# Interleaving the operation streams of attention and of the recurrent and SSD groups, with separate PSUM banks, in a two-layer hybrid decoder

## Chip, cores and metric

One Trainium2 chip, all 8 NeuronCores, each working on two of the 16 sequences with no communication. The metric is the device time of the slowest core in microseconds; less is better.

## The reference

The model has two layers over x of shape (16, 4096, 1024), float32. Each layer mixes tokens and then channels.

```python
proj = h @ w_in[l]          # 1024 -> 4368 columns, split among three head groups
# A recurrent group: GeLU gate * RG-LRU(causal width-4 conv), 512 channels:
#   a = exp(-8 r softplus(-lam)); u = sqrt(1 - a^2) * (i * x);  h_t = a_t h_(t-1) + u_t
# B Mamba-2 SSD group: conv + SiLU, 16 heads of 64, state 128, chunks of 128:
y_diag = einsum('bgcls,bcsghp->bclghp', cb[:, :, None] * decay, x)
states = einsum('bclgn,bclghp->bcghpn', bc, x * decay_states[..., None])
y_off = einsum('bclgn,bcghpn->bclghp', cc, prev) * out_decay[..., None]
#   then + D x, * SiLU(z), RMSNorm by group, 1024 channels
# C attention: window 128, 8 query and 2 key/value heads of 64, one sink per head:
p = exp(logits - m); probs = p / (sum(p) + exp(sink - m)); out = probs @ vv
# the three outputs (2048 columns) go through w_out, then
h = layer_norm(alpha * h + mix)
# PEER: top-16 of 128^2 experts for each of 8 heads, gated GELU neurons
h = layer_norm(alpha * h + peer(h))
```

## The kernel before

Every operation is recorded in one program-wide list by `Prog.op`, with the names of what it reads and writes. From these names come the waits: an operation waits on the semaphore of the engine that made what it reads, and of the last readers of what it overwrites. PSUM is also tracked by bank: `bank_of` maps names to banks, a reader waits for the bank's last matmul, and a matmul waits for all readers of its bank since then. `emit` gives each engine its operations in the order in which they were recorded, so each of the five queues (PE, DVE, ACT, POOL, SP) runs in program order.

After an initial normalization and a conversion of the expert tables, each layer has a mixer phase (`mixer_phase`, L319) and a PEER phase (`peer_phase`, L593), with a barrier between them. The change lies in the mixer phase alone. It goes over 2 sequences of 32 chunks of 128 tokens, that is 64 chunks for each layer, and each chunk does these steps, in this order on every engine:

1. The chunk of h is loaded (L415), cast (L416), transposed on PE (L418) and copied (L419). The load overwrites the single buffer `h`, which L587 of the chunk before reads, and its SP queue stands behind the store L590.
2. Projections (L425 to L446), their copies, SiLU of z (L449, L450), softplus for dt (L452 to L455).
3. Attention, L457 to L483: for each of 8 heads two logit matmuls (L461, L462) into bank 5 or 6, mask (L464, DVE), maximum (L465), scaling and negation (L466, L467), a memset of the sum (L468), Exp with accumulated sum (L469, ACT), Exp of the sink (L470, ACT), sum and reciprocal (L471, L472), two transposes into bank 7 (L474), their copy (L475, ACT), two matmuls with v into bank 4 (L478, L479), and the scaled copy (L480, DVE). Most small buffers (`lm`, `pb`, `pTt`, columns of `sm`) are single. Then four transposes (L482) and a copy into ymT (L483).
4. Causal convolution (L487 to L491): 64 DVE operations on 16 blocks of 128 channels.
5. RG-LRU (L493 to L520), four blocks one after the other: cast (L495), gate matmuls (L498) into bank 5 or 6, Tanh (L499, L500), a DVE chain (L501 to L508), Ln and Exp (L509, L510), scan (L513), the gate's GeLU with POOL (L515 to L517) and Tanh (L518), and the product (L519, L520). ACT loads a function table where Ln and Tanh follow each other.
6. SiLU of the 12 SSD blocks (L523 on ACT, L524 on DVE, one buffer `th`), transposes (L526, L529) into bank 7, and small steps (L531 to L542).
7. SSD for each of two groups (L543 to L578): decay matrix through fp32 matmuls (L548) into banks 2 and 3, mask (L551, POOL), Exp (L552), product (L554), matmuls (L557) into bank 0 or 1, L560 into bank 4 or 6, L553 and L562 into bank 5, state update, gating, RMSNorm. Then transposes L580 and copy L581.
8. Output projection (L585) into banks 0 and 1, residual (L587), LayerNorm (`ln_rows`, L257), store (L590).

Of the kernel before, what the change touches and what calls it, by code (L numbers as in the profile page):

```python
# [22 lines left out]
class Prog:  # L23
# [161 lines left out]
def bc(ap, shape):  # L185
    return ap.to_broadcast(list(shape))
# [132 lines left out]
def mixer_phase(nc, P, es_outer, E, l):  # L319
    op = P.op  # L320
    g = E
    NSEQ, S, NCH = g["NSEQ"], g["S"], g["NCH"]
    PB, PT = g["PB"], g["PT"]
    ident, iof, triu, ones, smask, amask, AMK = g["ident"], g["iof"], g["triu"], g["ones"], g["smask"], g["amask"], g["AMK"]
    hs0, hs1 = g["hs0"], g["hs1"]
    lnst, ln_rows, epsb = g["lnst"], g["ln_rows"], g["epsb"]
    with contextlib.ExitStack() as st:
# [4 lines left out]
        Wg = sb("Wg", [128, 4, 2, 128], BF16)  # L332
# [3 lines left out]
        rgc = sb("rgc", [128, 4, 4])  # L336
# [65 lines left out]
        PTv = PT[:].rearrange("p (k e) -> p k e", k=8)  # L402

        for sq in range(NSEQ):
# [6 lines left out]
            for c in range(NCH):  # L411
# [44 lines left out]

                for hd in range(8):  # L457
# [28 lines left out]

                for b in range(16):  # L487
                    eng = "dve"
                    op(eng, lambda e, b=b: e.tensor_scalar(out=xc[:, b, :], in0=X[:, b, 0:128], scalar1=cw[:, b, 0:1], scalar2=cw[:, b, 4:5], op0=ALU.mult, op1=ALU.add), reads=["X", "Xh0", "cw"], writes=[("xc", b), "wgs"])
                    for k in range(1, 4):  # L490
                        op(eng, lambda e, b=b, k=k: e.scalar_tensor_tensor(out=xc[:, b, :], in0=X[:, b, k:k + 128], scalar=cw[:, b, k:k + 1], in1=xc[:, b, :], op0=ALU.mult, op1=ALU.add), reads=["X", "Xh0", "cw", ("xc", b)], writes=[("xc", b)])  # L491

                for b in range(4):  # L493
                    A, B_, C_, D_, E_, F_, G_, H_ = [t1[i] for i in range(8)]
                    op("act", lambda e, b=b: e.copy(out=xcb[:], in_=xc[:, b, :]), reads=[("xc", b)], writes=["xcb"])  # L495
                    bk = 5 + b % 2
                    for gi in range(2):
                        op("pe", lambda e, b=b, gi=gi, bk=bk: e.matmul(PB[bk][:, gi * 128:(gi + 1) * 128], lhsT=Wg[:, b, gi, :], rhs=xcb[:], start=True, stop=True), reads=["Wg", "xcb"], writes=[("lg", bk, gi)])  # L498
                    op("act", lambda e, b=b, bk=bk: e.activation(out=A[:], in_=PB[bk][:, 0:128], func=AF.Tanh, bias=rgc[:, b, 0:1], scale=0.5), reads=[("lg", bk, 0), "rgc"], writes=["tA", ("seg", 0), ("seg", 1)])  # L499
                    op("act", lambda e, b=b, bk=bk: e.activation(out=B_[:], in_=PB[bk][:, 128:256], func=AF.Tanh, bias=rgc[:, b, 1:2], scale=0.5), reads=[("lg", bk, 1), "rgc"], writes=["tB", ("seg", 0), ("seg", 1)])  # L500
# [42 lines left out]
                for g_ in range(2):  # L543
# [9 lines left out]
                    op("pe", lambda e, g_=g_: e.matmul(PB[5][:, 0:128], lhsT=xsb[:, 8 + g_, :], rhs=xsb[:, 10 + g_, :], start=True, stop=True), reads=[("xsb", 8 + g_), ("xsb", 10 + g_)], writes=["pb5", ("lg", 5, 0)])  # L553
                    op("dve", lambda e: e.tensor_tensor(out=MT[:], in0=seg[:], in1=bc(PB[5][:, 0:128].unsqueeze(1), [128, 8, 128]), op=ALU.mult), reads=[("seg", 0), ("seg", 1), "pb5"], writes=["MT"])  # L554
# [353 lines left out]
```

How the kernel before makes its waits and increments, by code:

```python
            def run(engname, eng):  # L134
                waited = {}
                for o in ops:
                    if o["eng"] != engname:
                        continue
                    need = {}
                    for d in o["deps"]:
                        s, v = semval(ops[d])
                        key = id(s)
                        if need.get(key, (None, 0))[1] < v:
                            need[key] = (s, v)
                    for key, (s, v) in need.items():
                        if waited.get(key, 0) >= v:
                            continue
                        waited[key] = v
                        eng.wait_ge(s, v)
                    ins = o["fn"](eng)
                    if o["dma"] is not None:
                        lst = ins if isinstance(ins, (list, tuple)) else [ins]
                        assert len(lst) == o["ndma"], (len(lst), o["ndma"])
                        s, _ = semval(o)
                        for x in lst:
                            x.then_inc(s, 16)
                    elif o["sig"]:
                        s, _ = semval(o)
                        ins.then_inc(s, 1)
                if engname == "sp":
                    for n, s in dsem.items():
                        eng.wait_ge(s, self.dma_cum[n])
```

## Time and profile before

| | |
|---|---|
| median of 3 runs | 64667.56 us (64598.34 to 64866.73) |
| profiled execution, its own time | 64709.24 us |
| its span, slowest core (core 1) | 64707.7 us |
| spans of all cores | 64189.3 to 64707.7 us |
| busy PE / DVE / ACT / POOL, core 1 | 27332.0 / 28776.0 / 21378.7 / 10896.5 us (42% / 44% / 33% / 17%) |

The span is the time from the first to the last instruction of the core. A busy share is an average over phases that have different limits, so it is read by stretch. The granted clock is the share of TensorE's full clock of 2.4 GHz that was granted; 0.50 is the lower level of 1.2 GHz.

### The profile page before, as it was taken

The page shows a single profiled execution, that of the slowest core. Times are in us where ns is not written, and L with a number is a line of the kernel's source. Part 1 is how long each engine was busy: PE and PEld are TensorE (multiplying, and loading weights), DVE is VectorE, ACT ScalarE, POOL GpSimd, SP SyncE. Part 2 cuts the span into 40 slices and gives each one's busy share as a digit, 9 for nine tenths or more (in the row PEclk, how much of TensorE's full clock was granted, in tenths as well). Part 3 has the DMA queues.
Part 4 walks back from the last instruction along what each step waited for, and adds up shares of the span by engine and source line. Part 5 has one row for each costly group of instructions (what it writes and reads, how often), then busy time and mean ns, then how long its engine had stood idle before and what let it go on. Part 6 is the DMA issues. An engine that isn't in the chain of part 4 may idle for free.

```text
span 64707.7 us, 666132 instructions; the slowest of 8 cores (64189.3 to 64707.7 us)
## 1 busy us (share of the span) xinstructions
PE 27332.0 (42%) x192896; PEld 17066.1 (26%) x192896; DVE 28776.0 (44%) x65858; ACT 21378.7 (33%) x30175; POOL 10896.5 (17%) x12169
## 2 busy tenths in 40 slices
PE   0122222222456565555562222222245555565556
PEld 0011111111233333333331111111123333333333
DVE  1033333433555555555543433333455555555554
ACT  0122222222344444444432222222234444444444
POOL 2111111111121222222221111111112221222222
PEclk9955555555676777777775555555567777777778
DMA  3500000000233333333340000000023333333334
GB/s 130 179 5 6 6 6 6 5 6 6 88 129 129 129 131 131 131 130 132 131 149 15 5 6 6 6 6 6 5 71 130 131 132 130 131 131 131 131 134 152
DMA packets 2497687, 5211.34 MB, mean 81 GB/s; under 512 B 155808, under 2 KB 155808, under 8 KB 2490016
## 3 DMA queue, kind: packets, MB, share of 16 engines
q1 hardware_dynamic: 2494112, 5168.71, 23.6%
q8 instruction: 1629, 26.69, 0.2%
q14 instruction: 1946, 15.94, 0.1%
HBM read 4866.33 MB, written 301.99 MB: 80 GB/s over the span
## 4 chain that ended last, share of the span: by engine, by line
PE 28%; DVE 28%; ACT 18%; issue 11%; DMA 9%; POOL 4%; DVEq 1%; SPq 1%; ACTq 0%; POOLq 0%
PE pb L821 8%; ACT WT_p L782 8%; PE pb L831 7%; DMA Ug_p<-UTs 5%; DVE xc L491 3%; PE pb L425 3%; PE pb L585 2%; DMA ust<-peer_u 2%; PE pb L548 1%; PE pb L675 1%; DVE seg L505 1%; DVEq L149 1%; ACT ge_p L822 1%; ACT L509 1%; ACT L518 1%
## 5 line engine op out<-in xcount | busy, mean ns | idle before, releaser
L821 PE MATMUL pb<-h1T_p,Ug_p 128*128 128x256 bf16 x65536 | 9784.6, 318 | 8077.9 <-ACT ge_p L822 5328.6
L823 POOL TENSOR_TENSOR gW_p<-ge_p,WT_p 128x256 bf16<-128x256 bf16 x8192 | 6310.7, 777 | 26455.2 <-ACT ge_p L822 19428.0
L821 PEld LDWEIGHTS pb<-h1T_p,Ug_p 128*128 128x128 bf16 x65536 | 7139.9, 112 | 10467.3 <-issue 8751.7
L831 PE MATMUL pb<-Vg_p,gW_p 128*128 128x512 bf16 x32768 | 8657.7, 425 | 4.4 <-DMA Vg_p<-VBs 4.2
L822 ACT ACTIVATE ge_p<-pb 128x256 bf16<-128x256 f32 x8192 | 3341.5, 421 | 8694.4 <-PE pb L821 7202.8
L782 ACT CAST WT_p<-pt 128x512 bf16<-128x512 f32 x2048 | 5000.2, 2441 | 1567.7 <-PE pb L780 1508.8
L768 DVE TENSOR_TENSOR ohA_p<-iocb,selT_p 128x1024 bf16<-128x1024 bf16 x2048 | 2626.3, 1282 | 5981.3 <-PE pb L780 3181.7
L782 ACT CAST WT_p<-pb 128x512 bf16<-128x512 f32 x2048 | 4988.3, 2436 | 241.7 <-PE pb L831 3.4
L770 DVE TENSOR_TENSOR ohB_p<-iocb,selT_p 128x2048 bf16<-128x2048 bf16 x2048 | 4876.3, 2381 | 0.0
L831 PEld LDWEIGHTS pb<-Vg_p,gW_p 128*128 128x128 bf16 x32768 | 3462.1, 107 | 4335.2 <-issue 2627.7
L498 PE MATMUL pb<-xcb,Wg 128*128 128x128 bf16 x1024 | 190.5, 289 | 6615.7 <-ACT xcb L495 6615.7
L769 DVE TENSOR_TENSOR ohA_p<-ohA_p,selT_p 128x1024 bf16<-128x1024 bf16 x2048 | 2758.1, 1347 | 219.7 <-DVE ohA_p L768 8.3
L841 DVE SCALAR_TENSOR_TENSOR sc_p<-hq_p,pb 128x512 f32<-128x512 f32 x256 | 176.1, 688 | 5796.0 <-PE pb L831 4912.8
L515 POOL TENSOR_TENSOR seg<-gate 128x128 f32<-128x128 f32 x512 | 203.9, 398 | 14675.5 <-DVE ymT L520 12874.1
L491 DVE SCALAR_TENSOR_TENSOR xc<-X,cw,xc 128x128 f32<-128x128 f32 x6144 | 2158.4, 351 | 659.2 <-DVE xc L491 14.2
L693 DVE MAX8 V_p<-sc_p 128x8 f32<-128x128 f32 x2048 | 567.4, 277 | 3107.1 <-ACT sc_p L685 3105.7
L498 PEld LDWEIGHTS pb<-xcb,Wg 128*128 128x128 bf16 x1024 | 69.8, 104 | 6736.5 <-issue 6736.5
L548 PE MATMUL pb<-daU,ones 128*128 128x512 f32 x1024 | 941.1, 1074 | 2012.6 <-DVE daU L546 2012.6
L474 PE MATMUL pt<-ident,pb 128*128 128x128 bf16 x2048 | 379.9, 288 | 3337.5 <-ACT pb L469 3337.5
L425 PE MATMUL pb<-hT,Wi 128*128 128x128 bf16 x25600 | 1720.4, 238 | 121.9 <-DVE hT L419 121.9
L425 PEld LDWEIGHTS pb<-hT,Wi 128*128 128x128 bf16 x25600 | 1701.7, 108 | 152.3 <-issue 152.3
L780 PE MATMUL pt<-ohA_p,ohB_p 128*128 128x64 bf16 x16384 | 974.5, 210 | 1145.1 <-DVE ohB_p L770 1101.4
(244 smaller groups left out, 42165.5 us busy)
## 6 DMA issues: line engine op xcount, KB each, us to landing
Ug_p<-UTs SPq DMA_DIRECT2D x2048, 1024.0 KB, 8.2
Vg_p<-VBs SPq DMA_DIRECT2D x2048, 1024.0 KB, 5.5
ust<-peer_u SPq DMA_DIRECT2D x256, 512.0 KB, 4.0
vst<-peer_v SPq DMA_DIRECT2D x256, 512.0 KB, 4.8
hq_p<-hs SPq DMA_DIRECT2D x256, 512.0 KB, 6.2
UTs<-utb SPq DMA_DIRECT2D x256, 256.0 KB, 2.1
VBs<-vbf SPq DMA_DIRECT2D x256, 256.0 KB, 2.6
h<-hs SPq DMA_DIRECT2D x128, 512.0 KB, 3.8
```

The source lines that it names most:

```text
L425: op("pe", lambda e, b=b, c0=c0, kc=kc: e.matmul(PB[bank][:, b * 128:(b + 1) * 128], lhsT=Wi[:, kc, c0:c0 + 128], rhs=hT[:, kc, :], start= ...
L491: op(eng, lambda e, b=b, k=k: e.scalar_tensor_tensor(out=xc[:, b, :], in0=X[:, b, k:k + 128], scalar=cw[:, b, k:k + 1], in1=xc[:, b, :], o ...
L548: op("pe", lambda e, j=j: e.matmul(PB[2 + j][:, :], lhsT=ones[:], rhs=daU[:, 4 * j:4 * j + 4, :].rearrange("p a b -> p (a b)"), start=True ...
L585: op("pe", lambda e, hf=hf, kc=kc: e.matmul(PB[hf][:, :], lhsT=ymT[:, kc, :], rhs=Wo[:, kc, 512 * hf:512 * (hf + 1)], start=(kc == 0), sto ...
L768: op("dve", lambda e: e.tensor_tensor(out=ohA[o_][:], in0=ioh, in1=bc(selT[sl][:, 0, toks].unsqueeze(2), [128, 16, 64]), op=ALU.is_equal), ...
L769: op("dve", lambda e: e.tensor_tensor(out=ohA[o_][:], in0=ohA[o_][:], in1=bc(selT[sl][:, 2, toks].unsqueeze(2), [128, 16, 64]), op=ALU.mul ...
L770: op("dve", lambda e: e.tensor_tensor(out=ohB[o_][:], in0=iob, in1=bc(selT[sl][:, 1, toks].unsqueeze(2), [128, 16, 128]), op=ALU.is_equal) ...
L782: op("act", lambda e, tk0=tk0, dst_ps=dst_ps: e.copy(out=WT[:, i0c, tk0:tk0 + 8].rearrange("p i t -> p t i"), in_=dst_ps[:, :].rearrange(" ...
L821: op("pe", lambda e, gl=gl, kc=kc, ab=ab: e.matmul(PB[ab][:, 0:TT], lhsT=Ug[gs_][:, gl, kc, :], rhs=h1T[sl][:, kc, :], start=(kc == 0), st ...
L822: op("act", lambda e, ab=ab: e.activation(out=ge[ab][:], in_=PB[ab][:, 0:TT], func=AF.Gelu), reads=[("pp", ab)], writes=[f"ge{ab}"])
L823: op("pool", lambda e, ab=ab, gl=gl, eb=eb: e.tensor_tensor(out=gW[gs_][:, gl, :], in0=ge[ab][:], in1=WT[:, eb, :], op=ALU.mult), reads=[f ...
L831: op("pe", lambda e, gl=gl, sub=sub, hf=hf, bk=bk: e.matmul(PB[bk][:, :], lhsT=gW[gs_][:, gl, sub * 128:(sub + 1) * 128], rhs=Vg[gs_][:, g ...
```

## The change

Three things are done.

`Prog` gets a recording mode: while `chain` is a list, `op` only appends its arguments to it. `merge(a, b)` then records two such lists into the program, taking from the one that is behind in proportion of its length; the order inside each list stays. The dependencies are worked out at this point, in the merged order.

In `mixer_phase`, steps 3 (attention, with L482 and L483) go into `_chA`, and steps 4 to 7 (convolution to L581) into `_chB`; after L581 the two are merged. Steps 1, 2 and 8 stay outside.

The PSUM banks of `_chB` change. Gate matmuls L498: bank 5 or 6 to bank 0. Transposes L526, L529 and L580: bank 7 to bank 1, through a bf16 view `PT1`. L531 and L532: bank 6 to 3. L553: bank 5 to 0. L557: bank `g_` to 1 for both groups. L560: bank 4 or 6 to 2. L562: bank 5 to 3. L548 keeps banks 2 and 3, and attention its banks 4 to 7. The instructions that read these banks are changed alike, and so are the names by which waits are found. No operation is added or taken away.

```diff
+    chain = None
+
+    def merge(self, a, b):
+        na, nb = len(a), len(b)
+        ia = ib = 0
+        while ia < na or ib < nb:
+            if ib >= nb or (ia < na and ia * nb <= ib * na):
+                self.op(*a[ia]); ia += 1
+            else:
+                self.op(*b[ib]); ib += 1
+
     def op(self, eng, fn, reads=(), writes=(), dma=None, ndma=1):
+        if self.chain is not None:
+            self.chain.append((eng, fn, tuple(reads), tuple(writes), dma, ndma))
+            return None
...
+        PT1 = PB[1][:].bitcast(BF16)
+        PT1v = PT1.rearrange("p (k e) -> p k e", k=8)
...
+                _chA = []
+                P.chain = _chA
                 for hd in range(8):
...
+                _chB = []
+                P.chain = _chB
...
-                    bk = 5 + b % 2
+                    bk = 0
                     for gi in range(2):
-                        op("pe", lambda e, b=b, gi=gi, bk=bk: e.matmul(PB[bk][:, gi * 128:(gi + 1) * 128], lhsT=Wg[:, b, gi, :], rhs=xcb[:], start=True, stop=True), reads=["Wg", "xcb"], writes=[("lg", bk, gi)])
-                    op("act", lambda e, b=b, bk=bk: e.activation(out=A[:], in_=PB[bk][:, 0:128], func=AF.Tanh, bias=rgc[:, b, 0:1], scale=0.5), reads=[("lg", bk, 0), "rgc"], writes=["tA", ("seg", 0), ("seg", 1)])
...
-                op("pe", lambda e: e.matmul(PB[6][:, 0:16], lhsT=triu[:], rhs=s16(1), start=True, stop=True), reads=["triu", "da"], writes=["pcs"])
...
+                op("pe", lambda e: e.matmul(PB[3][:, 0:16], lhsT=triu[:], rhs=s16(1), start=True, stop=True), reads=["triu", "da"], writes=[("pbz", 1)])
...
-                        op("pe", lambda e, hh=hh, hcol=hcol, g_=g_: e.matmul(PB[g_][:, hh * 64:(hh + 1) * 64], lhsT=MT[:, hh, :], rhs=xdt[:, hcol], start=True, stop=True),
-                           reads=["MT", "xdt"], writes=[("pb", g_, hh // 2)])
-                    yo = 4 if g_ == 0 else 6
+                        op("pe", lambda e, hh=hh, hcol=hcol, g_=g_: e.matmul(PB[1][:, hh * 64:(hh + 1) * 64], lhsT=MT[:, hh, :], rhs=xdt[:, hcol], start=True, stop=True),
+                           reads=["MT", "xdt"], writes=[("pb", 1, hh // 2)])
+                    yo = 2
...
+                P.chain = None
+                P.merge(_chA, _chB)

```

## Rows read from the trace of the kernel before

**Rows 1.** Cores: span of a core, granted clock.

```profile
core 1: 64707.7 us, clock 0.680
...
die 1 (median of its cores): 64232.7 us, clock 0.702
```

**Rows 2.** The stores of the first mixer phase: durations in ns, first and last start.

```profile
L590 SPq DMA_DIRECT2D hs<-y x64: 319/320/332, 3471.3 to 16466.7; - x64
```

**Rows 3.** Windows of one chunk, core 1: busy time of each engine, clock, DMA.

```profile
10098.00:10132.00 34.00, 7.34 (x46) 3.09 (x46) 14.41 (x65) 9.27 (x32) 0.00 (x0) 0.50 0.00 1
10132.00:10158.00 26.00, 0.96 (x6) 0.48 (x6) 20.99 (x65) 2.90 (x5) 0.00 (x0) 0.50 0.00 1
10158.00:10195.00 37.00, 1.12 (x6) 0.41 (x6) 19.87 (x72) 18.12 (x34) 3.44 (x9) 0.50 0.00 0
10195.00:10204.00 9.00, 2.12 (x8) 0.83 (x8) 3.42 (x12) 3.10 (x11) 0.00 (x0) 0.50 0.00 0
10204.00:10252.00 48.00, 11.66 (x36) 4.85 (x36) 16.74 (x26) 9.04 (x19) 16.45 (x11) 0.57 0.00 0
10252.00:10274.40 22.40, 11.01 (x40) 4.57 (x40) 4.01 (x7) 1.51 (x3) 4.85 (x3) 0.65 0.00 1
```

**Rows 4.** Timeline of the first attention head: start us, us, what, idle before.

```profile
10098.03 0.42 DVE L464 TENSOR_TENSOR lm<-pb,amask 128x256 f32<-128x256 f32 x1
...
10099.51 0.06 DVE L468 MEMSET sm<- 128x1 f32 x1
...
10099.68 0.51 ACT L469 ACTIVATE pb<-lm,sm 128x256 bf16<-128x256 f32 x1 [1.86 <-DVE sm L468]
...
10100.89 0.37 ACT L475 COPY pTt<-pt 128x256 bf16<-128x256 bf16 x1 [0.42 <-PE pt L474]
...
10102.21 0.42 DVE L464 TENSOR_TENSOR lm<-pb,amask 128x256 f32<-128x256 f32 x1
```

**Rows 5.** Timeline of DVE where attention ends and the convolution begins.

```profile
10132.11 0.34 DVE L489 TENSOR_SCALAR xc<-X,cw 128x128 f32<-128x128 f32 x1
10132.56 1.27 DVE L491 SCALAR_TENSOR_TENSOR xc<-X,cw,xc 128x128 f32<-128x128 f32 x3
10133.75 0.34 DVE L489 TENSOR_SCALAR xc<-X,cw 128x128 f32<-128x128 f32 x1
```

**Rows 6.** Timeline of the recurrence, end of block 0 and start of block 1.

```profile
10164.50 1.28 ACT L518 ACT_TABLE_LOAD   x1
...
10164.98 0.48 DVE L513 TENSOR_TENSOR_SCAN lru<-seg,lst 128x128 f32<-128x128 f32 x1
...
10165.80 0.31 ACT L518 ACTIVATE seg<-seg 128x128 f32<-128x128 f32 x1
10166.01 0.28 ACT L495 CAST xcb<-xc 128x128 bf16<-128x128 f32 x1
10166.21 0.29 DVE L519 SCALAR_TENSOR_TENSOR seg<-seg,gate 128x128 f32<-128x128 f32 x1 [0.49 <-ACT seg L518]
...
10167.37 0.37 ACT L500 ACTIVATE seg<-pb,rgc 128x128 f32<-128x128 f32 x1
...
10167.76 0.31 ACT L502 ACTIVATE seg<-seg 128x128 f32<-128x128 f32 x1
```

**Rows 7.** Timelines: the last transposes of attention, SiLU, SSD group 1.

```profile
10132.34 0.59 PE L482 MATMUL pt<-ident,yc 128*128 128x128 bf16 x4 [0.54 <-DVE yc L480]
...
10133.01 0.59 ACT L483 COPY ymT<-pt 128x512 bf16<-128x512 bf16 x1 [1.73 <-PE pt L482]
...
10203.19 0.31 ACT L523 ACTIVATE th<-xc 128x128 f32<-128x128 f32 x1 [0.54 <-DVE xsb L524]
...
10235.44 0.69 DVE L549 TENSOR_TENSOR seg<-pb,sm 128x512 f32<-128x512 f32 x1 [2.30 <-PE pb L548]
```

**Rows 8.** Timeline of ACT ahead of attention.

```profile
10093.82 1.09 ACT L449 ACTIVATE gz<-pb 128x512 f32<-128x512 f32 x2
10096.00 0.23 ACT L453 ACTIVATE sm<-sm 128x16 f32<-128x16 f32 x1 [1.09 <-DVE sm L452]
10096.30 1.28 ACT L454 ACT_TABLE_LOAD   x1
```

More of the change, by code:

```diff
@@ L525, in mixer_phase @@
                 for kc in range(8):
-                    op("pe", lambda e, kc=kc: e.transpose(out=PT[:, kc * 128:(kc + 1) * 128], in_=xsb[:, kc, :], identity=ident[:]), reads=[("xsb", kc), "ident"], writes=[("pt", kc)])
-                op("act", lambda e: e.copy(out=xtm[:], in_=PT[:]), reads=[("pt", k) for k in range(8)], writes=["xtm"])
+                    op("pe", lambda e, kc=kc: e.transpose(out=PT1[:, kc * 128:(kc + 1) * 128], in_=xsb[:, kc, :], identity=ident[:]), reads=[("xsb", kc), "ident"], writes=[("pb", 1, kc)])
@@ L528, in mixer_phase @@
+                op("act", lambda e: e.copy(out=xtm[:], in_=PT1), reads=[("pb", 1, k) for k in range(8)], writes=["xtm"])
                 for j in range(2):
-                    op("pe", lambda e, j=j: e.transpose(out=PT[:, j * 128:(j + 1) * 128], in_=xsb[:, 8 + j, :], identity=ident[:]), reads=[("xsb", 8 + j), "ident"], writes=[("pt", j)])
-                op("act", lambda e: e.copy(out=btm[:], in_=PTv[:, 0:2, :]), reads=[("pt", 0), ("pt", 1)], writes=["btm"])
-                op("pe", lambda e: e.matmul(PB[6][:, 0:16], lhsT=triu[:], rhs=s16(1), start=True, stop=True), reads=["triu", "da"], writes=["pcs"])
@@ L532, in mixer_phase @@
-                op("pe", lambda e: e.matmul(PB[6][:, 16:32], lhsT=ones[:], rhs=s16(1), start=True, stop=True), reads=["ones", "da"], writes=["ptot"])
-                op("dve", lambda e: e.tensor_copy(out=s16(3), in_=PB[6][:, 0:16]), reads=["pcs"], writes=["cs"])
-                op("dve", lambda e: e.tensor_copy(out=s16(4), in_=PB[6][:, 16:32]), reads=["ptot"], writes=["tot"])
+                    op("pe", lambda e, j=j: e.transpose(out=PT1[:, j * 128:(j + 1) * 128], in_=xsb[:, 8 + j, :], identity=ident[:]), reads=[("xsb", 8 + j), "ident"], writes=[("pb", 1, j)])
@@ new lines, in mixer_phase @@
+                op("act", lambda e: e.copy(out=btm[:], in_=PT1v[:, 0:2, :]), reads=[("pb", 1, 0), ("pb", 1, 1)], writes=["btm"])
+                op("pe", lambda e: e.matmul(PB[3][:, 0:16], lhsT=triu[:], rhs=s16(1), start=True, stop=True), reads=["triu", "da"], writes=[("pbz", 1)])
+                op("pe", lambda e: e.matmul(PB[3][:, 16:32], lhsT=ones[:], rhs=s16(1), start=True, stop=True), reads=["ones", "da"], writes=[("pbz", 1)])
+                op("dve", lambda e: e.tensor_copy(out=s16(3), in_=PB[3][:, 0:16]), reads=[("pbz", 1)], writes=["cs"])
@@ L535, in mixer_phase @@
+                op("dve", lambda e: e.tensor_copy(out=s16(4), in_=PB[3][:, 16:32]), reads=[("pbz", 1)], writes=["tot"])
                 op("act", lambda e: e.activation(out=s16(5), in_=s16(3), func=AF.Exp), reads=["cs"], writes=["ea"])
@@ L552, in mixer_phase @@
                     op("act", lambda e: e.activation(out=seg[:], in_=seg[:], func=AF.Exp), reads=[("seg", 0), ("seg", 1)], writes=[("seg", 0), ("seg", 1)])
-                    op("pe", lambda e, g_=g_: e.matmul(PB[5][:, 0:128], lhsT=xsb[:, 8 + g_, :], rhs=xsb[:, 10 + g_, :], start=True, stop=True), reads=[("xsb", 8 + g_), ("xsb", 10 + g_)], writes=["pb5", ("lg", 5, 0)])
-                    op("dve", lambda e: e.tensor_tensor(out=MT[:], in0=seg[:], in1=bc(PB[5][:, 0:128].unsqueeze(1), [128, 8, 128]), op=ALU.mult), reads=[("seg", 0), ("seg", 1), "pb5"], writes=["MT"])
+                    op("pe", lambda e, g_=g_: e.matmul(PB[0][:, 0:128], lhsT=xsb[:, 8 + g_, :], rhs=xsb[:, 10 + g_, :], start=True, stop=True), reads=[("xsb", 8 + g_), ("xsb", 10 + g_)], writes=[("pb", 0, 0)])
@@ L562, in mixer_phase @@
-                    op("pe", lambda e, g_=g_, cols=cols: e.matmul(PB[5][:, :], lhsT=btm[:, g_, :], rhs=xds[:, cols], start=True, stop=True), reads=["btm", "xds"], writes=["pb5", ("lg", 5, 0), ("lg", 5, 1)])
+                       reads=[("xsb", 10 + g_), "ssb"], writes=[("pbz", 0)])
+                    op("pe", lambda e, g_=g_, cols=cols: e.matmul(PB[3][:, :], lhsT=btm[:, g_, :], rhs=xds[:, cols], start=True, stop=True), reads=["btm", "xds"], writes=[("pbz", 1)])
                     sv = ssf[:, cols].rearrange("p (h d) -> p h d", h=8)
@@ L564, in mixer_phase @@
                     op("pool", lambda e, sv=sv, hs_=hs_: e.tensor_tensor(out=sv, in0=sv, in1=bc(s16(7)[:, hs_].unsqueeze(2), [128, 8, 64]), op=ALU.mult), reads=["ssf", "cd"], writes=["ssf"])
-                    op("dve", lambda e, cols=cols: e.tensor_tensor(out=ssf[:, cols], in0=ssf[:, cols], in1=PB[5][:, :], op=ALU.add), reads=["ssf", "pb5"], writes=["ssf"])
+                    op("dve", lambda e, cols=cols: e.tensor_tensor(out=ssf[:, cols], in0=ssf[:, cols], in1=PB[3][:, :], op=ALU.add), reads=["ssf", ("pbz", 1)], writes=["ssf"])
@@ L566, in mixer_phase @@
                     yv = y1[:, cols].rearrange("p (h d) -> p h d", h=8)
-                    op("dve", lambda e, yv=yv, yo=yo, hs_=hs_: e.tensor_tensor(out=yv, in0=PB[yo][:, :].rearrange("p (h d) -> p h d", h=8), in1=bc(s16(5)[:, hs_].unsqueeze(2), [128, 8, 64]), op=ALU.mult), reads=[("yoff", g_), "ea"], writes=[("y1", g_), "ho"])
-                    op("act", lambda e, g_=g_, cols=cols: e.copy(out=ssb[:, cols], in_=ssf[:, cols]), reads=["ssf", ("yoff", g_)], writes=["ssb"])
-                    op("dve", lambda e, g_=g_, cols=cols: e.tensor_tensor(out=y1[:, cols], in0=y1[:, cols], in1=PB[g_][:, :], op=ALU.add), reads=[("y1", g_)] + [("pb", g_, b) for b in range(4)], writes=[("y1", g_)])
+                    op("dve", lambda e, yv=yv, yo=yo, hs_=hs_: e.tensor_tensor(out=yv, in0=PB[yo][:, :].rearrange("p (h d) -> p h d", h=8), in1=bc(s16(5)[:, hs_].unsqueeze(2), [128, 8, 64]), op=ALU.mult), reads=[("pbz", 0), "ea"], writes=[("y1", g_), "ho"])
@@ L570, in mixer_phase @@
+                    op("act", lambda e, g_=g_, cols=cols: e.copy(out=ssb[:, cols], in_=ssf[:, cols]), reads=["ssf", ("pbz", 0)], writes=["ssb"])
+                    op("dve", lambda e, g_=g_, cols=cols: e.tensor_tensor(out=y1[:, cols], in0=y1[:, cols], in1=PB[1][:, :], op=ALU.add), reads=[("y1", g_)] + [("pb", 1, b) for b in range(4)], writes=[("y1", g_)])
                     op("pool", lambda e, cols=cols, hs_=hs_: e.tensor_tensor(out=y2[:, cols].rearrange("p (h d) -> p h d", h=8), in0=xtm[:, cols].rearrange("p (h d) -> p h d", h=8), in1=bc(dsk[:, hs_].unsqueeze(2), [128, 8, 64]), op=ALU.mult), reads=["xtm", "dsk"], writes=[("y2", g_), ("r1", 0), ("r1", 1)])
@@ L579, in mixer_phase @@
                 for kc in range(8):
-                    op("pe", lambda e, kc=kc: e.transpose(out=PT[:, kc * 128:(kc + 1) * 128], in_=yb[:, kc * 128:(kc + 1) * 128], identity=ident[:]), reads=[("yb", 0), ("yb", 1), "ident"], writes=[("pt", kc)])
-                op("act", lambda e: e.copy(out=ymT[:, 4:12, :], in_=PTv), reads=[("pt", k) for k in range(8)], writes=["ymT_b"])
+                    op("pe", lambda e, kc=kc: e.transpose(out=PT1[:, kc * 128:(kc + 1) * 128], in_=yb[:, kc * 128:(kc + 1) * 128], identity=ident[:]), reads=[("yb", 0), ("yb", 1), "ident"], writes=[("pb", 1, kc)])
+                op("act", lambda e: e.copy(out=ymT[:, 4:12, :], in_=PT1v), reads=[("pb", 1, k) for k in range(8)], writes=["ymT_b"])
+                P.chain = None
+                P.merge(_chA, _chB)
                 YK = ["ymT_b", "ymT_c"] + [("ymT_a", b) for b in range(4)]
```

6 lines of the change are left out of this document (4 added, 2 removed).

## The prediction

> **What bounds the kernel now.** I read the cores first: the slowest, core 1, spans 64707.7 us, and the other die is only 0.7% shorter [rows 1], so one core stands for all. The page splits this span into a mixer and a PEER phase for each of two layers; the change touches only the mixer. There the store of each chunk is a clock: 64 of them lie between 3471.3 and 16466.7 us, so a chunk takes 12995.4 / 63 = 206.3 us [rows 2], and there are 2 layers x 64 = 128 chunks, 26.4 ms in all. Next I cut one chunk (207.7 us) into stretches [rows 3]. In none of them is an engine full, the convolution apart (DVE 20.99 of 26 us). The attention stretch is 34.0 us with DVE 14.41, ACT 9.27, PE 7.34 and POOL 0 busy: a head goes from engine to engine, and each waits for the last. The timelines say it head by head: L464 of head 0 starts at 10098.03, that of head 1 at 10102.21 [rows 4], and the first L489 of the convolution at 10132.11 [rows 5]. So attention takes 34.08 us, 4.26 a head, and everything after it waits, though it needs none of its results before the output projection. The chain that sets the end runs through all these stretches in turn.
>
> **What the change removes.** These 34.08 us as a stretch of their own. No arithmetic goes. The new bank names take away every PSUM bank that both streams used: attention keeps banks 4 to 7, the recurrent/SSD stream has 0 to 3. Inside that stream the shared banks cost nothing: each next writer (gates of the next block in bank 0, L557 of the second group in bank 1, L548 in banks 2 and 3 after L567 and L565) already stands behind its reader in the DVE or ACT order of before. DMAs are untouched: the only two a chunk issues stand outside the merged part.
>
> **What it adds.** Counting the calls, attention has 141 operations and the other stream 306, so one attention operation follows each 2 or 3 of the other (2.17 on average), by count and not by time. That puts 29 (1.7 heads) into the convolution, 55 (3.25 heads) into the recurrence, 11 (0.65) into SiLU, 11 (0.6) into the transposes and small steps, 30 (1.8) into the SSD groups and 5 behind. Engines keep program order, so each costs what it delays the stream behind it. The terms, per chunk:
>
> *Convolution, 2.0 us.* All on DVE, a chain: an L491 follows the one it needs every 0.45 us, and the independent L489 starts before its predecessor has ended [rows 5]. An attention operation between two dependent ones fills that gap, so it costs its duration less about 0.2 us: nothing for the four or five of 0.06 to 0.21 us in a head, 0.2 each for L464 and L465 (0.42 us) [rows 4]. Low end 1.7 x 0.5 = 0.9; high end all of DVE's attention work, 1.7 x 14.41 / 8 = 3.1. I take the middle. PE and ACT are idle here [rows 3], and a head's slot is some 15 us for 4.26 us of latency, so DVE never waits for it.
>
> *Recurrence, 6.5 us.* Four blocks of about 9.5 us. What matters is ACT's order. In block 0 the Exp L469 of head 2 stands on ACT between L510 and the table load of L518, and needs L468, which is on DVE behind the scan L513 (to 10165.46). The load now starts at 10164.50 under that scan [rows 6]; it would start after the scan, the 0.06 us reset, a hop of 0.1 and Exp with its accumulator read (0.60), near 10166.3: 1.8 us late, with 0.5 more on DVE before it. In block 1, L464 to L467 fill DVE behind L512 (0.7 us more than the wait they replace), and and then L469 stands on ACT before L499 while its L468 is still behind L520 on DVE: together 1.4 on the way to L501, and 0.3 for an L470 between L518 and L495 (0.28), 1.7 in all. Block 2: an L471 that waits for L470, and L465 to L467 ahead of L501: 1.2. Block 3: an L475 ahead of the load and small ones: 0.7. That is 5.9, and 0.6 for operations inside the DVE chain. Low end 1.7 (only the first load late); high end fully serial, 3.25 x 4.26 = 13.8.
>
> *SiLU, 0.4.* ACT and DVE take turns with 0.5 us of idle each [rows 7], which holds an L464. Low 0, high 0.65 x 4.26 = 2.8.
>
> *Small steps, 1.7.* The eighth transpose L526 comes behind an L478 which waits for an L475 that waits on ACT behind the last Tanh: 0.4 + 0.2 + 0.4 = 1.0; L464 and L465 stand in the chain to L541: 0.5; rest 0.2. Low 0.5, high 0.6 x 4.26 = 2.6.
>
> *SSD and the end, 1.4.* The chain moves through long steps; DVE waits 2.3 us for the first pair of L548 [rows 7], ACT and PE longer, and the attention operations sit in these waits; 0.4 for transposes between the L557. The four L482 (0.59 us) and copy L483 (0.59) now stand in front of L581 [rows 7]: 1.0. Low 0.9, high 1.8 x 4.26 + 1 = 8.7.
>
> Sum 2.0 + 6.5 + 0.4 + 1.7 + 1.4 = 12.0 (ends: 4.0 and 31.0). Saved: 34.1 - 12.0 = 22.1 us a chunk, x 128 = 2829 us. The profiled execution took 64709.2 us (span 64707.7), 42 above the median of the runs; 64709 - 2829 - 42 = 61,840 us, 4.4% faster.
>
> **A price that could undo this: tables.** An added table load costs 1.28 us [rows 6]. Here Exp L453 follows Tanh L449 without a load, though Ln L454 needs one [rows 8], and Exp L469 follows that Ln without one [rows 4]; L502 follows L500 likewise [rows 6]. So attention's Exp fits whichever table is in place, and I count no new load. The Trainium skill, ScalarE: Activation LUTs, section Table sets, tells to batch activations by set and not to mix them, which speaks against this interleaving; but its list puts exp beside both tanh and ln, and by that, as by the rows, the sum is unchanged.
>
> **The rivals.**
> 1. *Queues in lockstep (slower).* Each hop of a head stalls the other stream, and the operations of that stream, between those of attention, stall the head in turn. For it: block 0 above, where one operation of 0.5 us costs 1.8. Against it: hops are only 0.1 to 0.2 us [rows 4], and a slot of 17 operations lasts 11 us or more. It decides when a head costs more than 4.26 us of delay; at the price of block 0 at each of the three points where a head comes onto ACT, 8 x 3 x 1.8 = 43.2 us, +9.1 a chunk: 65.8 ms. Chance 3%.
> 2. *Shared engines.* What attention occupies on DVE and ACT lands on the chain whole: 14.41 + 9.27 = 23.7 us; saved 10.4, 1.33 ms: 63.3 ms. For it: in convolution and recurrence DVE and ACT are the chain. Against it: the idle DVE and ACT time in SiLU and SSD. 16%.
> 3. *Table loads.* One load for each head's Exp pair and one back, 16 x 1.28 = 20.5 us: saved 1.6, 64.4 ms, no change that can be told. 2%.
> 4. *The clock gives more.* The recurrence, SiLU and, mostly, the SSD stretch have the granted clock at 0.50 to 0.57, the lower level of 1.2 GHz, and the stretch with L585 only 0.65 [rows 3]; PE is hardly busy in them. With attention's matmuls spread in, a rise that comes earlier would shorten PE's 11.66 + 11.01 us there by up to a third, 6 to 7 us: 61.0 ms. The attention stretch speaks against: PE busy 7.34 of 34 us, and still 0.50. 8%. The Trainium skill, TensorE: Matmul & The Clock Gate, section HAM oscillation, says idle gaps bring the clock down; the trace agrees so far that it is low after idle stretches.
> 5. *No effect,* the chain being elsewhere: the 128 stretches leave no room for it. 1%.
>
> **How the numbers follow.** The forecast itself has 70%; its own range, with 8 to 18 us of cost, is 61.3 to 62.6 ms. Runs of this kernel agree such that about 0.5% can be told from no change. Faster by more than that: the forecast, rivals 2 and 4, 94%; same 3%; slower 3%. Rivals 2 and 4 reach to 63.3 and 61.0; leaving out 2 in 10 gives 61,100 to 63,000 us.
>
> **What would show it.** Right: chunk period near 184 us; PEER phases as before; no more ACT_TABLE_LOADs; in the convolution DVE nearly full and some 2 us longer; in recurrence block 0 the load of L518 behind L469; SSD stretches near their 48 us. A period near 196 with DVE and ACT waits spread out is rival 2; more table loads rival 3; L585 at short durations from its first matmul rival 4. The prediction is wrong above all if queue stalls in the recurrence or around L557 are larger than walked here, since they were followed by order and not measured.

## The result, and the profile after

The changed kernel takes 61441.7 us (median of 8 runs, 61319.7 to 61616.8) where the kernel before takes 64713.4 (8 runs): a ratio of 0.9493, 95% interval 0.9477 to 0.9509. That is 5.1% faster; forecast were 61,840 us, or 4.4%, and a range of 61,100 to 63,000. Its lines below L58 have moved by 14 to 22: attention's L464 to L480 are now L482 to L498, the recurrence's L509, L513 and L518 are L529, L533 and L538, SSD's L548 is L568, the store L590 is L612.

First the store of each chunk in the first mixer phase, as in [rows 2], on core 3, now the slowest (durations in ns, first and last start):

```profile
L612 SPq DMA_DIRECT2D hs<-y x64: 319/320/332, 3465.1 to 14830.3; - x64
```

The period of a chunk is (14830.3 - 3465.1) / 63 = 180.4 us, where it was 206.3: 25.9 less, x 128 = 3313 us (in the second layer's mixer phase it is 180.8, where it was 206.5). The profiled executions differ by 64709.2 - 61304.5 = 3405, 92 more. From the last store of the first mixer phase to the first of the second, which is PEER and one more chunk, it was 17867.7 us on core 1 before and is 17774.4 on core 3 now, and core 3 had 17783.8 before. The eight cores of the one execution before differ in this stretch by 271 us, three times the 92 (17596.4 to 17867.7), so those 92 are not put down to the change. The gain lies in the mixer.

One chunk, cut where convolution, recurrence, SiLU, small steps, SSD and end begin (windows of core 3; busy time of PE, PEld, DVE, ACT, POOL, then clock and DMA):

```profile
9810.80:9838.10 27.30, 2.29 (x14) 0.94 (x14) 22.85 (x81) 4.54 (x12) 0.00 (x0) 0.50 0.00 0
9838.10:9879.70 41.60, 3.84 (x24) 1.69 (x24) 23.41 (x98) 21.04 (x46) 3.52 (x9) 0.50 0.00 1
9879.70:9888.90 9.20, 1.41 (x9) 0.86 (x9) 4.24 (x20) 4.23 (x15) 0.00 (x0) 0.50 0.00 0
9888.90:9894.80 5.90, 1.91 (x11) 1.46 (x11) 3.03 (x10) 2.11 (x6) 0.89 (x1) 0.50 0.00 0
9894.80:9937.70 42.90, 11.98 (x41) 4.86 (x41) 16.13 (x34) 9.02 (x21) 15.50 (x11) 0.54 0.00 0
9937.70:9960.50 22.80, 10.71 (x43) 4.73 (x43) 4.43 (x7) 2.00 (x4) 4.85 (x3) 0.65 0.00 1
```

The attention window of [rows 3], 34 us, has no counterpart: its instructions are in the counts of all the others. The clock is where it was: in the SSD window it is 0.54 here and 0.57 in [rows 3], but that is the scatter from chunk to chunk before (0.50 to 0.57). The mean over the chunks of this window is 0.54 in both traces.

The same cuts in one chunk of every trace give the table that the rest of this text works with. Each number is a time in us between two starts: of the first convolution operation, of the first DVE operation of the recurrence, of the first and the last SiLU product on DVE (L544 of the changed kernel), of the first DVE operation of SSD group 0 (L566), of the last RMSNorm product (L598), and of the first matmul of the output projection. "Sum" runs from the first of these to the last; attention's own stretch, where it runs alone, comes on top (34.1 us in the chunk of [rows 4], 33.8 by the median of all chunks of that trace; 33.5 in banks_only_b and 33.7 in the two filler kernels). A single chunk can be off by some 0.5 us, so the last but one column gives the median of the sum over all 128 chunks of the core. The period is that of the first mixer phase.

| kernel | convolution | recurrence | SiLU | small | SSD | end | sum | median sum | chunk period |
|---|---|---|---|---|---|---|---|---|---|
| before | 26.2 | 37.5 | 9.0 | 4.4 | 42.2 | 3.2 | 122.5 | 122.8 | 206.3 |
| changed | 27.2 | 41.6 | 9.2 | 5.9 | 42.9 | 3.7 | 130.5 | 130.5 | 180.4 |
| banks_only_b | 26.2 | 37.5 | 9.0 | 4.4 | 42.6 | 3.2 | 122.9 | 123.0 | 206.2 |
| late_only_b | 26.4 | 37.3 | 9.7 | 8.9 | 46.5 | 5.7 | 134.3 | 134.4 | 184.0 |
| early_only_b | 28.1 | 44.2 | 9.0 | 4.4 | 42.6 | 3.2 | 131.5 | 131.7 | 180.9 |
| placed_heads | 26.4 | 37.5 | 9.5 | 4.5 | 42.5 | 3.2 | 123.6 | 123.0 | 172.9 |
| conv_fill_small | 26.5 | 37.3 | 9.1 | 4.4 | 42.4 | 3.2 | 122.9 | 122.9 | 206.6 |
| conv_fill_large | 32.4 | 37.2 | 9.2 | 4.5 | 42.4 | 3.2 | 128.9 | 129.3 | 212.8 |
| small_banks_shared | 27.2 | 41.6 | 9.1 | 5.9 | 42.9 | 3.7 | 130.4 | 130.3 | 180.9 |
| hold_between_loads | 27.2 | 41.1 | 9.2 | 5.9 | 42.6 | 3.6 | 129.6 | 129.6 | 179.8 |

The change costs 130.5 - 122.5 = 8.0 us a chunk in the stretches that stay and removes 34.1: 26.1 net. By the medians it costs 7.7 and removes 33.8. The periods say 25.9.

How convolution takes an attention operation (timeline of DVE):

```profile
9812.49 0.34 DVE L509 TENSOR_SCALAR xc<-X,cw 128x128 f32<-128x128 f32 x1
9812.75 0.42 DVE L482 TENSOR_TENSOR lm<-pb,amask 128x256 f32<-128x256 f32 x1
9813.08 0.80 DVE L511 SCALAR_TENSOR_TENSOR xc<-X,cw,xc 128x128 f32<-128x128 f32 x2
...
9814.38 0.34 DVE L509 TENSOR_SCALAR xc<-X,cw 128x128 f32<-128x128 f32 x1
9814.64 0.20 DVE L484 TENSOR_SCALAR sm<-sm,snk 128x1 f32<-128x1 f32 x1
9814.83 0.81 DVE L511 SCALAR_TENSOR_TENSOR xc<-X,cw,xc 128x128 f32<-128x128 f32 x2
```

From an L509 to the L511 that needs it were 0.45 us [rows 5]. With the 0.42 us of L482 between them they are 0.59, with the 0.20 us of L484 still 0.45. In front of an L509, which needs nothing of the operation before it, there is no such gap to fill:

```profile
9829.56 0.41 DVE L483 TENSOR_REDUCE sm<-lm 128x1 f32<-128x256 f32 x1
9829.89 0.34 DVE L509 TENSOR_SCALAR xc<-X,cw 128x128 f32<-128x128 f32 x1
```

Without an operation between them an L509 follows the last L511 of the block before after 0.27 us; with an L483 it is 0.60, with a short operation of 0.15 us 0.34 (medians). Taken over all 128 chunks, the gaps give the convolution's whole cost: three long operations between dependent ones (0.44 us together), one long one in front of an L509 (0.33) and two short ones in front of one (0.14), 0.9 us by the median.

Block 0 of the recurrence, timelines of ACT and DVE, beside [rows 6]:

```profile
9844.64 0.31 ACT L530 ACTIVATE seg<-seg 128x128 f32<-128x128 f32 x1
...
9845.52 0.48 DVE L533 TENSOR_TENSOR_SCAN lru<-seg,lst 128x128 f32<-128x128 f32 x1
9845.95 0.06 DVE L486 MEMSET sm<- 128x1 f32 x1
...
9846.12 0.51 ACT L487 ACTIVATE pb<-lm,sm 128x256 bf16<-128x256 f32 x1 [1.17 <-DVE sm L486]
9846.54 0.19 ACT L487 ACTIVATION_READ_ACCUMULATOR pb<-lm,sm 128x1 f32 x1
9846.75 1.28 ACT L538 ACT_TABLE_LOAD   x1
...
9848.45 0.29 DVE L539 SCALAR_TENSOR_TENSOR seg<-seg,gate 128x128 f32<-128x128 f32 x1 [2.19 <-ACT seg L538]
```

ACT is idle for 1.17 us before L487, since L487's reset L486 stands behind the scan on DVE. The table load follows L487 at 9846.75; before, it followed L510 at once. DVE then waits 2.19 us for the Tanh, where it waited 0.49.

In block 1 a head delays the stream a second time, less. On DVE the reset L486 stands behind L540, on ACT the Exp stands in front of the next block's first Tanh (L499 before, L519 now). Before, and after:

```profile
10167.38 0.29 DVE L501 TENSOR_SCALAR seg<-seg,rgc 128x128 f32<-128x128 f32 x1 [0.48 <-ACT seg L499]
...
9859.19 0.29 DVE L540 SCALAR_TENSOR_TENSOR ymT<-seg,lru 128x128 bf16<-128x128 f32 x1
9859.60 0.51 ACT L487 ACTIVATE pb<-lm,sm 128x256 bf16<-128x256 f32 x1 [1.23 <-DVE sm L486]
9860.11 0.35 ACT L519 ACTIVATE seg<-pb,rgc 128x128 f32<-128x128 f32 x1
9860.57 0.29 DVE L521 TENSOR_SCALAR seg<-seg,rgc 128x128 f32<-128x128 f32 x1 [1.07 <-ACT seg L519]
```

No table load was added: L529 and L538 have 256 each and four other lines 64 each in the first mixer phase, as before.

```profile
L529 ACT ACT_TABLE_LOAD x256 | 328.4, 1283 | 936.5 <-DVE seg L528 928.8 <-DVE sm L484 4.2 <-DVE seg L531 3.5
L538 ACT ACT_TABLE_LOAD x256 | 328.4, 1283 | 4.6
L465 ACT ACT_TABLE_LOAD x64 | 82.1, 1283 | 1.1
L470 ACT ACT_TABLE_LOAD x64 | 82.1, 1283 | 4.9
L519 ACT ACT_TABLE_LOAD x64 | 82.1, 1283 | 1.2
L596 ACT ACT_TABLE_LOAD x64 | 82.1, 1283 | 21.5 <-DVE rn L595 21.5
```

### The profile page after: what moved, and what is told of

Its sections match the earlier page's. It is cut to its first block, busy times and chain, and to the rows that moved or that the text cites. A ratio compares the mean times of both kernels' runs of the same rounds, so it can differ in the third digit from the quotient of the medians.

```text
span 61303.0 us, 660243 instructions; the slowest of 8 cores (60921.3 to 61303.0 us)
## 1 busy us (share of the span) xinstructions
PE 26856.9 (44%) x192896; PEld 17074.3 (28%) x192896; DVE 28104.0 (46%) x65858; ACT 21265.7 (35%) x30175; POOL 10915.5 (18%) x12169
## 4 chain that ended last, share of the span: by engine, by line
PE 28%; DVE 26%; ACT 18%; issue 12%; DMA 9%; POOL 5%; DVEq 1%; SPq 1%; ACTq 0%; POOLq 0%
PE pb L843 9%; ACT WT_p L804 8%; PE pb L853 7%; DMA Ug_p<-UTs 5%; DVE xc L511 3%; PE pb L441 3%; PE pb L607 2%; DMA ust<-peer_u 2%; PE pb L568 2%; PE pb L697 1%; ACT ge_p L844 1%; ACT L529 1%; DVE I_p L719 1%; DVE I_p L716 1%; POOL seg L571 1%
## 5 line engine op out<-in xcount | busy, mean ns | idle before, releaser
L853 PE MATMUL pb<-Vg_p,gW_p 128*128 128x512 bf16 x32768 | 8432.6, 417 | 1.8 <-DMA Vg_p<-VBs 1.7
L511 DVE SCALAR_TENSOR_TENSOR xc<-X,cw,xc 128x128 f32<-128x128 f32 x6144 | 2153.1, 350 | 540.7 <-DVE xc L511 7.8
L487 ACT ACTIVATE pb<-lm,sm 128x256 bf16<-128x256 f32 x1024 | 516.4, 504 | 3864.5 <-DVE sm L486 3864.4
L568 PE MATMUL pb<-daU,ones 128*128 128x512 f32 x1024 | 950.7, 1084 | 1969.1 <-DVE daU L566 1270.2
L518 PE MATMUL pb<-xcb,Wg 128*128 128x128 bf16 x1024 | 190.3, 289 | 3529.1 <-ACT xcb L515 3528.7
L492 PEld LDWEIGHTS pt<-ident,pb 128*128 128x128 bf16 x2048 | 201.1, 119 | 4799.5 <-issue 4799.5
```

The source lines that it names most:

```text
L568: op("pe", lambda e, j=j: e.matmul(PB[2 + j][:, :], lhsT=ones[:], rhs=daU[:, 4 * j:4 * j + 4, :].rearrange("p a b -> p (a b)"), start=True ...
L853: op("pe", lambda e, gl=gl, sub=sub, hf=hf, bk=bk: e.matmul(PB[bk][:, :], lhsT=gW[gs_][:, gl, sub * 128:(sub + 1) * 128], rhs=Vg[gs_][:, g ...
```

## The experiments

The theory to test: all of the gain is the overlap of two streams, and what the merge costs is decided by position alone, that is by which operation stands in front of one that is needed sooner. Its main rival was the prediction's second, shared engines: attention's busy time lands on the chain wherever it is put. The first four kernels ran on one chip, where the kernel before took 64741.4 us, the other four on another, where it took 64351.9. Ratios are to these, so between kernels of different chips the ratios are compared and not the times. One kernel gave no time and is missing below: the merge with the old banks, in which both streams write the same columns of banks 4 to 7. So no run shows what the merge costs without separate banks.

### The banks without the merge

```diff
-                P.merge(_chA, _chB)
+                for _o in _chA + _chB:
+                    P.op(*_o)
```

> The new banks without the merge: attention first, then the other stream, as before. My theory (the gain is the overlap of the two streams, and the shared banks cost nothing while they run one after the other): a chunk period of 206 us and 64.7 ms, within 0.3% of the kernel before. A rival, that part of the gain comes from the new banks themselves (waits for a bank's old reader that are gone): 3 us or more less per chunk, below 64.3 ms.

Measured: 64774.0 us, ratio 1.000 (0.9987 to 1.0012), period 206.2. The new banks alone give nothing, as expected. That they matter because they let the merge be made is argued from the code, where without them each stream would overwrite the other's data.

### Attention merged with the later part only

```diff
-                P.merge(_chA, _chB)
+                for _o in _chB[:_nL]:
+                    P.op(*_o)
+                P.merge(_chA, _chB[_nL:])
```

`_nL` is the number of operations of convolution and recurrence.

> Attention's 141 operations are merged only with the SiLU, small, SSD and end part (122 operations, 59 us of a chunk); the convolution and the recurrence run alone. My theory (an attention operation costs only where it stands before an operation that is needed sooner): convolution and recurrence return to 26.0 and 37.2 us, which gives back 5.7 us; the small steps, 4.4 us long, now hold 1.6 heads of 4.26 us and grow by 4 to 6, the SSD part with 4.5 heads by 2 to 5: 61.3 to 62.2 ms. The rival that attention's busy time on DVE and ACT adds wherever it lands: 23.7 us a chunk of cost, 63.3 ms.

Measured: 61914.4 us, ratio 0.9553 (0.9534 to 0.9571). Convolution and recurrence are back at 26.4 and 37.3. The small steps grew by 4.5 and SSD by 4.3, both inside what was expected; SiLU by 0.7, the end by 2.5, which was not listed apart. The cost is 11.8 us (11.6 by the medians), half of the 23.7 that the rival asks for.

### Attention merged with the early part only

```diff
-                P.merge(_chA, _chB)
+                P.merge(_chA, _chB[:_nL])
+                for _o in _chB[_nL:]:
+                    P.op(*_o)
```

> Attention's 141 operations are merged only with convolution and recurrence (184 operations, 63 us), the rest runs alone. My theory: convolution with 2.9 heads costs 2 us, the recurrence with 5.1 heads 6 to 10, since more heads come onto ACT between the two table loads; the later part returns to its old length (1.6 less in small steps, 1 less at the end): 61.5 to 62.2 ms. The rival of the added busy time: 63.3 ms.

Measured: 61662.8 us, ratio 0.9521 (0.9504 to 0.9539). Convolution 1.9 longer for 2.9 heads, recurrence 6.7 for 5.1 heads, both as expected, the rest as before: 9.0 us with 0.4 of scatter in SSD, 8.9 by the medians. The ratio is a little worse than its period of the first mixer phase says: in the second the period is 183.0 on this core (181.1 and 181.3 on two of the other die), since the stretch from the output projection to the next convolution takes 2.5 us longer there, at a granted clock of 0.71 against 0.77. In both halves a head costs far less than the 3.0 us of DVE and ACT that it keeps busy (23.7 / 8): 0.66 us in the convolution and 1.3 in the recurrence.

### Heads placed by hand

The same streams and banks, but a list says before which operation of the recurrent/SSD stream how many of attention's have been recorded. The core of the list, with comments of this text (17 operations a head; `q` is the first operation of a recurrence block):

```python
for b in range(4):
    k, q = 17 * b, 64 + 30 * b
    m[q + 17] = k + 2          # the two logit matmuls
    m[q + 21] = k + 7          # mask .. reset on DVE, while ACT loads its table for Ln
    if b < 3:
        q += 30                # in the next block:
        m[q + 7] = k + 9       # the two Exp on ACT, under the DVE chain
        m[q + 11] = k + 10
        m[q + 12] = k + 16     # transposes, copy, matmuls with v
        m[q + 16] = k + 17
...                            # the rest of the fourth head: among SiLU and after
# in an SSD group, head one: (0, 2), (2, 9), (4, 11), (6, 16), (8, 17)
#                  head two: (9, 2), (20, 9), (28, 16), (29, 17)
```

> The changed kernel with the same two streams and banks, but attention's operations placed by hand where the trace shows the engine waiting, not by count: none in the convolution; one head in each block of the recurrence, its L464 to L468 on DVE while ACT loads the table ahead of L509, its ACT and PE operations under the DVE chain of the next block; two heads in each SSD group, in the waits for L548 and for L557. My theory (cost comes only from an operation standing in front of one that is needed sooner): the merged part costs 2 us a chunk, not 8.3, so 0.8 ms less than the changed kernel: 60.6 ms (60.3 to 61.0). The rival that the 8.3 us are the shared engines' busy time, wherever it is put: no gain, 61.3 to 61.7 ms.

Measured: 60581.8 us, ratio 0.9352 (0.9333 to 0.9371), 6.5% faster than before. The period is 172.9 us: of the 34 us of attention's stretch 33.4 are gone. The sum of the stretches is 123.6 in the chunk of the table, but its median over all chunks is 123.0, only 0.2 above that of before. The blocks of the recurrence have the lengths of before by their medians (9.25, 9.50, 9.49 and 8.93 us, before 9.26, 9.50, 9.50 and 8.93). In the timeline of one (here L521 to L525 are mask to reset, L568 and L569 Ln and Exp, L572 the scan, L577 the Tanh; L570 and L571 are the L511 and L512 of before, whose row stands first):

```profile
10164.58 0.29 DVE L512 SCALAR_TENSOR_TENSOR seg<-seg 128x128 f32<-128x128 f32 x1 [1.98 <-ACT seg L510]
...
9922.16 0.28 DVE L570 SCALAR_TENSOR_TENSOR seg<-seg,xc 128x128 f32<-128x128 f32 x1
9922.32 1.28 ACT L568 ACT_TABLE_LOAD   x1 [2.49 <-DVE seg L567]
9922.36 0.42 DVE L521 TENSOR_TENSOR lm<-pb,amask 128x256 f32<-128x256 f32 x1
...
9923.83 0.06 DVE L525 MEMSET sm<- 128x1 f32 x1
9924.02 0.31 ACT L569 ACTIVATE seg<-seg 128x128 f32<-128x128 f32 x1
9924.35 1.28 ACT L577 ACT_TABLE_LOAD   x1
9924.43 0.29 DVE L571 SCALAR_TENSOR_TENSOR seg<-seg 128x128 f32<-128x128 f32 x1 [0.54 <-ACT seg L569]
```

The five DVE operations of a head fit between L570 and L571, where DVE had been idle for 2 us and still is for 0.54, and the second table load follows L569 at once. Each engine has the same instructions as in the changed kernel (65858 on DVE, 30175 on ACT). So the 8.0 us (7.7 by the medians; the expectation has 8.3) were positions and not the busy time that was added, and the rival of shared engines falls. The list takes attention out of the convolution, and the Exp out of the place in front of the load and of the Tanh, at once; this run does not tell their shares apart.

### Short operations in the convolution's gaps

```diff
+                        op("dve", lambda e: e.memset(fil[:, 0:1], 0.0), writes=["fil"])
                         op(eng, lambda e, b=b, k=k: e.scalar_tensor_tensor(out=xc[:, b, :], ...
```

> The kernel before with 48 more DVE memsets of one element (0.06 us each) in each chunk, one in front of each L491 of the convolution. My theory: between two dependent operations DVE has a gap that an independent short one fills for nothing: no more than 0.5 us a chunk, 64.7 ms (within 0.2%). The rival that each operation adds at least its duration and an issue slot of 0.1 us: 5 us a chunk, 65.3 ms.

Measured: 64368.0 us, ratio 1.0004 (0.9994 to 1.0013). 48 more instructions a chunk, 6144 in all, cost nothing that can be told.

### The same with operations of 0.42 us

Against the kernel of the experiment above:

```diff
-                        op("dve", lambda e: e.memset(fil[:, 0:1], 0.0), writes=["fil"])
+                        op("dve", lambda e: e.reduce_max(out=fil[:, 0:1], in_=lm[:], axis=AX.X), reads=["lm"], writes=["fil"])
```

> The same with 48 maxima over 256 columns, as long as attention's L465 (0.42 us), in place of the memsets. In the prediction an operation between two dependent ones cost its duration less 0.2 us: 0.2 each, 9.6 us a chunk, 65.9 ms. The trace of the changed kernel shows an L483 to add only 0.14 to the 0.45 us from one L511 to the next: 6.7 us a chunk, 65.6 ms. The rival that durations add whole: 20 us a chunk, 67.3 ms.

Measured: 65168.7 us, ratio 1.0128 (1.0111 to 1.0145). 816.8 us more, / 128 = 6.4 a chunk, / 48 = 0.13 each. The timeline shows it:

```profile
9920.21 0.33 DVE L493 SCALAR_TENSOR_TENSOR xc<-X,cw,xc 128x128 f32<-128x128 f32 x1
9920.47 0.41 DVE L492 TENSOR_REDUCE fil<-lm 128x1 f32<-128x256 f32 x1
9920.80 0.34 DVE L493 SCALAR_TENSOR_TENSOR xc<-X,cw,xc 128x128 f32<-128x128 f32 x1
```

From one L493 to the next 0.59 us with the filler, where dependent ones follow every 0.45: in these rows each instruction starts some 0.08 us before the one in front of it ends, if it does not need it. The prediction's 0.2 for such an operation was 0.07 too much.

### Small uses of attention's banks

```diff
-                    bk = 0
+                    bk = 5 + b % 2
...
-e.matmul(PB[bk][:, gi * 128:(gi + 1) * 128], lhsT=Wg[:, b, gi, :], ... writes=[("pb", 0, gi)])
+e.matmul(PB[bk][:, 256 + gi * 128:256 + (gi + 1) * 128], lhsT=Wg[:, b, gi, :], ... writes=[("lg", bk, 2 + gi)])
```

> The changed kernel, but the gates (L518), L551, L552 and L573 are back in attention's banks 5 and 6, in columns that attention leaves free, with all waits by bank. My theory: the two streams' uses of these banks are short and rarely meet, so the waits cost under 1 us a chunk: 61.4 to 61.6 ms, as the changed kernel. The rival, that decoupling the banks is a large part of the gain: 2 us a chunk or more, over 61.7 ms.

Measured: 61098.8 us, ratio 0.9496 (0.9480 to 0.9512), against 0.9493 of the changed kernel (the expected times were for a chip on which the kernel before takes 64.7 ms). Waits by bank between the two streams cost nothing here, where the uses lie in different columns. That is a statement on these four uses only. Banks 4 and 7, and bank 5 for the matmul L582 that fills it whole, were not shared in a merged kernel.

### Nothing between the two table loads

```diff
-            if ib >= nb or (ia < na and ia * nb <= ib * na):
+            if ib >= nb or (ia < na and ia * nb <= ib * na and not ib in hold):
```

`hold` has the places of L530 to L538 of each block.

> The changed kernel, but no attention operation is put between L529 and L538 of a recurrence block; they come behind L538. My theory: in block 0 the table load of L538 is back under the scan and starts right after L530, 1.8 us earlier; the Exp then stands in front of the cast L515 and gives 0.6 to 1.0 us back, and operations bunched behind L538 take some in the other blocks: the recurrence, 41.6 us in the changed kernel, gets 0.5 to 1.5 us shorter. The rival, that the recurrence grew for DVE's added work: it stays at 41.6 or grows.

Measured: 60922.2 us, ratio 0.9467 (0.9448 to 0.9486; two runs), which overlaps with the changed kernel's. The trace decides. In block 0 the load is back behind L532, and the Exp comes behind the Tanh (timeline of ACT; L531 to L540 are the changed kernel's L529 to L538):

```profile
9813.31 0.31 ACT L532 ACTIVATE seg<-seg 128x128 f32<-128x128 f32 x1
9813.64 1.28 ACT L540 ACT_TABLE_LOAD   x1
9814.93 0.31 ACT L540 ACTIVATE seg<-seg 128x128 f32<-128x128 f32 x1
9815.43 0.51 ACT L487 ACTIVATE pb<-lm,sm 128x256 bf16<-128x256 f32 x1 [0.19 <-DVE sm L486]
```

The time from the block's first DVE instruction to the next block's fell from 11.75 to 10.74 us: 1.8 gained, 0.8 given back. The other three together lost 0.45, as operations bunched behind the Tanh. The recurrence is 0.55 shorter (0.6 by the medians, 41.7 to 41.1), the low end of what was expected: that the Exp held up the load is shown, and moving operations only behind the load is a poor cure for it.

## Why the prediction held, step by step

**The chain and what is removed.** Right. 34.1 us were the stretch in the chunk that was read (33.8 by the median), and it is gone as a stretch. From the first matmul of the output projection to the next attention or convolution it was 49.6 us and is 50.1, the stretch with PEER differs by less than it does between cores, and the 128 periods account for 3313 of the 3405 us.

**The banks.** Right as far as tested: no cost inside the stream and no gain without the merge (banks_only_b). What shared banks would cost in the merge is shown for four small uses only (small_banks_shared: nothing).

**The cost of 12.0 us a chunk.** The step that was mis-sized. It measured 8.0 in the chunk of the table and 7.7 by the medians:

| term | predicted | one chunk | median of 128 |
|---|---|---|---|
| convolution | 2.0 | 1.1 | 0.9 |
| recurrence | 6.5 | 4.1 | 4.3 |
| SiLU | 0.4 | 0.1 | 0.1 |
| small steps | 1.7 | 1.5 | 1.5 |
| SSD and end | 1.4 | 1.2 | 0.8 |

The convolution lies at the low end that the prediction gave, 0.9. A long operation between dependent ones costs 0.13 to 0.15, where 0.2 was counted, and what no row supported was to take the middle between this end and the whole busy time.

In the recurrence the block with the late table load was sized well: 2.3 predicted, 2.2 measured (its median length went from 9.26 to 11.48). The three blocks behind it were put at 1.7, 1.2 and 0.7 and cost 1.3, 0.5 and 0.2. In block 1 both delays are there and add up, as walked, but they are smaller: L540 comes 0.5 us later behind its load than L520 did, L519 waits 0.6 more for the Exp in front of it, 1.1 together instead of 1.4; and the Exp of the sink (L488), put at 0.3 in front of the cast, stands behind L520 there. In block 2, L489 waits 0.36 for L488, and L483 to L485 stand ahead of L521, as walked; but these three run for the most part while DVE would wait for ACT anyway (0.48 us before) and cost 0.38. In block 3 the copy L493 makes the load 0.26 late. The 0.6 that was added for operations inside the DVE chain was counted twice, since such operations are already in the 0.5 of block 0.

All five terms were put too high, so nothing cancelled: the time was met within 0.4 ms because the cost is small beside what is removed, and the range was wide. 12.0 - 7.7 = 4.3 us a chunk are 0.55 ms; the medians show 0.4 of it (61,840 forecast, 61,442 measured).

**The tables.** Right: no load was added, and the count by line shows it.

**The rivals.** Lockstep: a head stalls both streams in block 0, which the prediction named, and less in block 1; the two cost 2.2 and 1.3 us, far from 4.26 a head. Shared engines: it falls, most plainly by placed_heads, where the same instructions cost 0.2 us; only in the convolution, where DVE is nearly full, is a part of their duration paid. Table loads: none. The clock: the means over all chunks are 0.50 in convolution, recurrence, SiLU and small steps and 0.54 in SSD, before and after, and 0.75 from the output projection to the next chunk's attention or convolution, though 7 us of small matmuls are now spread over the merged stretches.

What stays open: whether a stream that shares banks 4 and 7 would lose the overlap, and how much of the 7.7 us each moved group of operations gives back in placed_heads.

## What to carry to other kernels

Two independent chains that each hop between engines with queues in program order could be merged here for almost nothing, but by position and not by count: put an operation where its engine already waits for another engine, and never a cross-engine wait in front of something long that could have started, such as a table load. On the trace, look for the idle time printed before each instruction of the main chain and fit the other chain's runs of work into it; here that took 7.7 us of cost to 0.2. A gap between two dependent operations on DVE is also room: an operation of up to 0.2 us fitted in for nothing, while in front of an independent one it cost 0.07.

One chunk is a sample. Where a reading rests on less than a microsecond, take the median over all chunks: one chunk of placed_heads showed 1.1 us of cost, 128 showed 0.2.

## What the runs showed of the hardware beyond expectation

In these traces DVE starts an instruction of the convolution some 0.08 us before the end of the one in front when it doesn't depend on it (L509 after 0.27 us), and 0.1 us after it when it does (L511 after 0.45); 6144 added memsets cost 0.04% (interval -0.06% to 0.13%), and 6144 operations of 0.42 us cost 0.13 us each. A table load shows as 1.28 us, and the next function starts 0.01 us behind it, with nothing visible between them in the rows above (9846.75 + 1.28 = 9848.03; the Tanh of L538 ran from 9848.04).
